# A fused two-block kernel: the low parts of the mixers' weights and three modulation vectors are made on GpSimd

## Time and profile before

| | |
|---|---|
| median of 3 runs | 1066.14 us (1065.88 to 1066.76) |
| the profiled execution | 1066.5 us, of which the span from first to last instruction is 1064.5 us |
| PE busy | 1027.7 us, 97% of the span |
| DVE busy | 700.2 us, 66% |
| ACT busy | 537.3 us, 50% |
| POOL busy | 39.0 us, 4% |
| DMA | 212.27 MB, mean 199 GB/s |

### The profile page before, as it was taken

One profiled execution on the slowest core, in us unless ns is written; L12 is line 12 of the kernel. 1 busy time (PEld: TensorE's weight loads), 2 busy tenths in 40 slices (PEclk: granted clock), 3 DMA queues, 4 the chain that ended last, 5 costly groups with the idle time before them and its releaser, 6 DMA issues.

```text
span 1064.5 us, 19831 instructions
## 1 busy us (share of the span) xinstructions
PE 1027.7 (97%) x8502; PEld 994.4 (93%) x8502; DVE 700.2 (66%) x1213; ACT 537.3 (50%) x903; POOL 39.0 (4%) x75
## 2 busy tenths in 40 slices
PE   5999999999988999999999999999999999999995
PEld 4899999988987899999999999999999999999985
DVE  3478886557687577776656778655457775555485
ACT  4453543455554655544444577554355554444453
POOL 5000000010000001000000000003000000000000
PEclk7999999999999999999999999999999999999998
DMA  9979889876734445577655456336156575565511
GB/s 304 380 251 318 310 319 322 287 247 204 212 109 159 157 144 155 197 244 271 205 191 183 135 178 218 120 123 175 60 163 216 187 237 164 194 198 163 195 40 40
DMA packets 144463, 212.27 MB, mean 199 GB/s; under 512 B 4259, under 2 KB 121239, under 8 KB 144376
## 3 DMA queue, kind: packets, MB, share of 16 engines
q1 hardware_dynamic: 138928, 194.40, 54.9%
q0 software_dynamic: 5184, 16.30, 4.8%
q10 hardware_dynamic: 264, 0.31, 0.1%
HBM read 209.88 MB, written 1.11 MB: 198 GB/s over the span
## 4 chain that ended last, share of the span: by engine, by line
PE 67%; issue 22%; DVE 7%; ACT 2%; DMA 1%; SPq 0%; POOL 0%; POOLq 0%; DVEq 0%; ACTq 0%
PE PS L460 65%; DVE wlo L1769 4%; PE PS L468 2%; DMA SC<-in_w_ada_dram 1%; ACT whi L1286 1%; DVE SC L1727 1%; DVE xT L1736 0%; DVE W L1727 0%; DVE hl L1736 0%; ACT SC L1278 0%; DVE st L1739 0%; DVE SC L1733 0%; DVE SS L1727 0%; ACT SC L1273 0%; DVE SC L2202 0%
## 5 line engine op out<-in xcount | busy, mean ns | idle before, releaser
L1769 DVE TENSOR_TENSOR wlo<-raw,whi 128x1024 fp32r<-128x1024 f32 (+2 forms) x331 | 386.8, 1186 | 203.2 <-ACT whi L1286 202.6
L1286 ACT ACTIVATE whi<-raw 128x1024 fp32r<-128x1024 f32 (+2 forms) x331 | 331.9, 1022 | 176.7 <-PE PS L460 137.7
L460 PE MATMUL PS<-hh,whi 128*128 128x256 f32 (+1 forms) x1376 | 393.8, 286 | 6.8 <-DVE wlo L1769 4.6
L460 PE MATMUL PS<-hh,wlo 128*128 128x256 f32 (+1 forms) x1376 | 388.6, 282 | 0.0
L460 PE MATMUL PS<-hl,whi 128*128 128x256 f32 (+1 forms) x1376 | 387.9, 282 | 0.0
L460 PE MATMUL PS<-SR,whi 128*128 128x256 f32 (+1 forms) x1824 | 329.1, 283 | 4.0 <-DVE wlo L1769 1.4
L460 PEld LDWEIGHTS PS<-SR,whi 128*128 128x128 f32 x1824 | 279.8, 188 | 8.9 <-issue 2.6
L460 PEld LDWEIGHTS PS<-hh,whi 128*128 128x128 f32 x1376 | 260.2, 189 | 12.8 <-DVE wlo L1769 6.5
L460 PEld LDWEIGHTS PS<-hl,whi 128*128 128x128 f32 x1376 | 261.0, 190 | 0.4
L460 PEld LDWEIGHTS PS<-hh,wlo 128*128 128x128 f32 x1376 | 260.8, 190 | 0.0
L460 PE MATMUL PS<-SR,wlo 128*128 128x256 f32 (+1 forms) x912 | 256.7, 281 | 0.0
(11 more groups left out here) (183 smaller groups left out, 714.5 us busy)
## 6 DMA issues: line engine op xcount, KB each, us to landing
raw<-in_ffn_w_dram SPq DMA_DIRECT2D x60, 1024.0 KB, 7.2
raw<-in_w_in_dram SPq DMA_DIRECT2D x38, 1024.0 KB, 5.4
raw<-in_w_ff_dram SPq DMA_DIRECT2D x32, 1024.0 KB, 5.3
raw<-in_w_ada_dram SPq DMA_DIRECT2D x16, 1024.0 KB, 6.6
SC<-in_w_ada_dram POOLq DMA_DIRECT2D x12, 1024.0 KB, 6.4
SC<-in_w_ada_dram SPq DMA_DIRECT2D x8, 1024.0 KB, 12.2
raw<-in_w_out_dram SPq DMA_DIRECT2D x8, 1024.0 KB, 4.9
raw<-in_ffn_w_dram SPq DMA_DIRECT2D x8, 768.0 KB, 12.6
```

Source lines behind the costliest of these rows:

```text
L460: return e.matmul(o, l, r, start=start, stop=stop, skip_group_check=True)
L1286: e.activation(hi_part(p), raw_part(p), ACT.Copy).then_inc(*hi_done.up(p.i))
L1769: e.tensor_tensor(lo_part(p), raw_part(p), hi32(hi_part(p)), ALU.subtract).then_inc(*lo_done.up(p.i))
```

## The change

- 113 of the 331 low parts are made by POOL, with the same subtraction: those of the first mixer from its third gate load on (43) and all of the second mixer (70). 103 of them are 128 x 1024, two are 128 x 768 and eight 128 x 256. They have a signal of their own, `lo_pool`. TensorE and SP wait for the one or the other by `low_signal`.
- Vectors 5, 6 and 7 are made on POOL as DVE makes 2, 3 and 4: for each row tile a multiplication by a column of `cact` in place, and an addition into `ada_buf[v]`, two instructions, of which the first tile of a vector needs only the multiplication. `pair_rows` is gone; TensorE does a `sum_rows` for each of the three.
- The loads of the pairs 2 to 11 are issued after the rows 0, 2, 4, ... of the first feed-forward (the last after row 18), and after POOL has used the slot.
- POOL's queue now holds, in order: constants and small loads; the twelve pairs, each with the load of the pair two later; a small memset; the low parts of the first mixer; the bias loads, with the low parts of the second mixer between them; the rest of the low parts; the last loads.

```
@@ -210,6 +209,7 @@
         for k in (0, 4):
             self.piece(c0, k, k + 4, 0, 256)
             self.piece(c1, k, k + 4, 0, 160)
+        self.on_pool = True
         for i in (2, 3, 4):
             self.tall("gate", w_in, GATE0 + 256 * i)
...
         self.row("out1", a["w_out"][0], 6)
+        self.on_pool = False
         for b in range(NB):
             self.block(1, w13[1], b)
...
+        self.on_pool = True
         for i in range(4):
             self.wide("qa", w_in2, QA + 256 * i)
...
         self.row("out2", a["w_out_2"][0], 6)
+        self.on_pool = False
         for j in range(18):
...
+        def low_signal(i):
+            return lo_pool if pieces[i].on_pool else lo_done
...
-                on.wait_ge(lo_done, p.i)
+                on.wait_ge(low_signal(p.i), p.i)
...
             def sum_rows(v, b, c):
-                on.wait_ge(dve_done, ("ada", v, 7))
+                on.wait_ge(pool_done if 5 <= v < 8 else dve_done, ("ada", v, 7))
...
-                if b > 6:
-                    pair_rows(5, b - 7, 7)
+                if b == 6:
+                    sum_rows(5, 7, 0)
...
-            on.wait_ge(dve_done, ("av", 0, 19))
-            pair_rows(6, 0, 5)
...
-            rows_end(todo, 0, lambda n: pair_rows(6, (n + 1) // 2, 5) if n in (1, 4, 6) else None)
+
+            def shift2_rows(n):
+                if n == 6:
+                    on.wait_ge(dve_done, ("av", 0, 19))
+                    sum_rows(6, 5, 0)
+
+            rows_end(todo, 0, shift2_rows)
...
-            on.wait_ge(dve_done, ("mean", 0))
-            for q in (0, 1):
-                pair_rows(7, q, 0)
...
-            for q in (2, 3):
-                pair_rows(7, q, 0)
+            on.wait_ge(dve_done, ("mean", 0))
+            sum_rows(7, 0, 0)
...
-            for n, u in enumerate(plan.rings["pair"]):
-                on.wait_ge(mm_done, plan.first_rows[5 + 2 * n].end if n < 2 else plan.rings["pair"][n - 2].end)
-                e.dma_start(ring_view(u), u.src).then_inc(*pair_in[u.slot].landed(u))
...
+            def lo_to(n):
+                while low["n"] < n:
+                    p = pieces[low["n"]]
+                    if p.on_pool:
+                        on.wait_ge(hi_done, p.i)
+                        e.tensor_tensor(lo_part(p), raw_part(p), hi32(hi_part(p)), ALU.subtract).then_inc(*lo_pool.up(p.i))
+                    low["n"] += 1
+
+            pairs = plan.rings["pair"]
+
+            def load_pair(n):
+                if n < 2:
+                    on.wait_ge(mm_done, plan.first_rows[5 + 2 * n].end)
+                else:
+                    on.wait_ge(mm_done, ("row", 0, 2 * n - 4 if n < 11 else NT - 4))
+                    on.wait_ge(pool_done, ("ada", 5 + (n - 2) // 4, 2 * ((n - 2) % 4) + 1))
+                e.dma_start(ring_view(pairs[n]), pairs[n].src).then_inc(*pair_in[pairs[n].slot].landed(pairs[n]))
+
+            load_pair(0)
+            load_pair(1)
+            on.wait_ge(act_done, "cact")
+            for n, u in enumerate(pairs):
+                v = 5 + n // 4
+                on.wait_ge(pair_in[u.slot], u)
+                for k in range(2):
+                    row = 2 * (n % 4) + k
+                    src, col, buf = ring_view(u)[:, k, :], cact[:, row:row + 1], ada_buf[v]
+                    if row:
+                        e.tensor_scalar(src, src, col, None, ALU.mult).then_inc(*pool_done.up(("times", v, row)))
+                        on.wait_ge(pool_done, ("times", v, row))
+                        e.tensor_tensor(buf, buf, src, ALU.add).then_inc(*pool_done.up(("ada", v, row)))
+                    else:
...
+                        e.tensor_scalar(buf, src, col, None, ALU.mult).then_inc(*pool_done.up(("ada", v, row)))
+                if n + 2 < len(pairs):
+                    load_pair(n + 2)
             on.wait_ge(dve_done, "rope", "axial")
             on.wait_ge(mm_done, ("ada_cols", 3))
             e.memset(cu[:, :, 0:2], 0.0).then_inc(*pool_done.up("pad"))
+            lo_to(split_at["acc", 1, 0][0])
...
                 if u >= 2:
+                    lo_to(split_at["s_b", u - 2][1])
                     on.wait_ge(dve_done, ("s_b", u - 2))
...
+            lo_to(len(pieces))
             on.wait_ge(dve_done, ("gm", 3, 7))
```

More of the change, by code:

```diff
@@ L113, with __init__ @@
 class Piece:
-    def __init__(self, i, load, k0, k1, c0, c1):
-        self.i, self.load, self.at, self.k, self.c = i, load, (k0, k1, c0, c1), k1 - k0, c1 - c0
+    def __init__(self, i, load, k0, k1, c0, c1, on_pool):
+        self.i, self.load, self.at, self.k, self.c, self.on_pool = i, load, (k0, k1, c0, c1), k1 - k0, c1 - c0, on_pool
 class Plan:
@@ L127, in __init__ @@
         self.rings = {"raw": [], "row": [], "pair": []}
-        self.first_rows, self.pairs = [], {}
+        self.first_rows, self.pairs, self.on_pool = [], {}, False
         self.lay_out(a)
@@ L137, in piece @@
     def piece(self, u, k0, k1, c0, c1):
-        self.pieces.append(Piece(len(self.pieces), u, k0, k1, c0, c1))
+        self.pieces.append(Piece(len(self.pieces), u, k0, k1, c0, c1, self.on_pool))
         u.end = ("lo", len(self.pieces) - 1)
@@ L562, in sum_rows @@
                 m.then_inc(*count(("ada_sum", v)))
[L564 to L571, removed]
             def sum_columns(vs, b):
@@ L1192, in sp_program @@
                     if old.end[0] == "lo":
-                        on.wait_ge(lo_done, old.end[1])
+                        on.wait_ge(low_signal(old.end[1]), old.end[1])
                     elif old.end[0] == "ada":
@@ L1386, in act_program @@
             hi_before(("ada_sum", 3))
-            ada_rows_out(5, 7, 0, ("pair", 5, 3), ("ada_sum", 4))
+            ada_rows_out(5, 7, 0, ("ada_sum", 4))
             ada_rows_out(4, 7, 256, ("ada_sum", 4))
@@ L1397, in act_program @@
                     on.wait_ge(dve_done, ("a", 0, NT - 1))
-                    ada_rows_out(6, 5, 0, ("pair", 6, 3))
+                    ada_rows_out(6, 5, 0, ("ada_sum", 6))
             hi_before(("g1", 0))
@@ L1410, in act_program @@
             hi_before("c_rows")
-            ada_rows_out(7, 0, 0, ("pair", 7, 3))
+            ada_rows_out(7, 0, 0, ("ada_sum", 7))
             on.wait_ge(mm_done, "c_rows", ("ada_col", 6))
@@ L1767, in lo_to @@
                         ada_sum()
-                    on.wait_ge(hi_done, p.i)
-                    e.tensor_tensor(lo_part(p), raw_part(p), hi32(hi_part(p)), ALU.subtract).then_inc(*lo_done.up(p.i))
+                    if not p.on_pool:
+                        on.wait_ge(hi_done, p.i)
+                        e.tensor_tensor(lo_part(p), raw_part(p), hi32(hi_part(p)), ALU.subtract).then_inc(*lo_done.up(p.i))
                     low["n"] += 1
@@ L2096, in dve_program @@
             last_one()
-            on.wait_ge(mm_done, ("pair", 7, 3))
             for t in range(2):
```

13 lines of the change are left out of this document (9 added, 4 removed).

## The result

The changed kernel takes 1116.75 us in the median of four runs (1114.66 to 1116.92), the kernel before 1066.2 us beside it: a ratio of 1.0469, 95% interval 1.0451 to 1.0487. The forecast was 1078 us and its range ended at 1092. It is slower by 50.6 us where 12 were forecast.

A forecast was written before the change was run, and what follows sets the result against it. The prediction took TensorE's work plus some 10 us of waits as the bound. It summed 1066.5 - 9.8 (pairs) + 16.6 (first feed-forward) + 0 + 5 (second mixer) = 1078.3, less 0.4 for the median: 1078 us, range 1048 to 1092.

The forecast's parts named there:

- Part 1: Twelve pairs leave TensorE and three row sums are added: net gain 9.8 us, 3.3 of it in the first feed-forward.
- Part 4, that the engines exclude each other: A POOL instruction reading SBUF and a two-SBUF-input DVE instruction exclude each other; the second is blocked until the first ends.
- Rival 1: Whole kernel: the engines don't hinder each other, so 1050 us, bounds 1047 and 1056; chance 0.34.
- rival 3: Second mixer: POOL is too slow for TensorE, over 2.86 us a low part; 1083 us at 3.3 us each; chance 0.07.
- Part 4, the first feed-forward: DVE's two-input work and POOL's 61.6 us exceed the 162.7 us stretch: 16.6 us lost, between 10.9 and 22.4.
- Part 5: Pair loads moved forward into the first feed-forward: cost 0, bound 4 us.
- Part 4, the second mixer: DVE's other work plus POOL's, 225.5 us for 218: 5 us lost, at least 0 and at most 7.5.
- Part 4, the first mixer: No lack of throughput, but small DVE steps can wait up to 2.2 us: 0, bounds of 5 either way.
- Part 2: POOL's prices: 1.1 us for one input, 2.2 us for two, so 6.6 us a pair and 61.6 us for ten.
- Rival 2: Whole kernel: partial hindrance, only some forms collide or they share by halves; about 1064 us, 1058 to 1068; chance 0.10.
- Rival 4: Relief of DVE is worth nothing outside the first mixer; alone, with the pairs' gain, 1056 us; chance counted in Rival 1.

The follow-up runs named there:

- Experiment 9: Experiment 1's kernel with each of POOL's multiplications and additions replaced by a memset of the same buffer: 1058.29 us, ratio 0.9916 to the kernel before.
- experiment 1: The changed kernel with all low parts back on VectorE, only the pairs (vectors 5, 6, 7) on POOL: 1082.0 us, ratio 1.0146 to the kernel before.
- experiment 8: The changed kernel with POOL's low parts cut into two halves (the eight of 128 x 256 stay whole): 1107.45 us, ratio 1.0397 to the kernel before.
- experiment 2: The kernel before with only the 113 low parts moved to POOL, the pairs still on TensorE: 1096.9 us, ratio 1.0285.

## Why the prediction was wrong, point by point

- **Part 1, the pairs leave TensorE, -9.8 us: right.** Experiment 9 has -9.0 us, 7.3 to 10.6. At its second milestone it is 7.1 us ahead: up to there TensorE waits 3.6 us in it, 1.4 before, so some 2 us of the gain come back as small waits.
- **Part 4, that the engines exclude each other: right in mechanism**, but for POOL's multiplication. Instructions of VectorE with two SBUF inputs grew beside POOL's reads, those with a PSUM input did not, and memsets did nothing. The Trainium skill ("SBUF — State Buffer", "Who interferes with whom") says the same of two-SBUF-input instructions, and that the fast mode of a one-input `tensor_scalar` contends as well; the 2851 ns beside 749 agree with it. The rule as the prediction gives it, that the one that comes second is blocked until the first has ended, holds here for POOL's subtractions and additions; beside its multiplications by a column VectorE was held up for about 1.0 of 2.85 us. Rival 1 (no hindrance, 1050 us) is false: VectorE's instructions did stretch. So is rival 3: 2.44 us a low part is below the 2.86 us of a piece, and nobody waited for POOL's low parts.
- **Part 4, the first feed-forward, +16.6 us: the number was right, 18.0 by experiments 1 and 9, but with luck.** It is a stretch bound by throughput: VectorE is busy 172.4 of 181 us. The sum took POOL's 61.6 us as its whole working time. But from 54 to 235 us of experiment 1 POOL ran 21 multiplications and 17 additions, 100 us even at their shortest (2.84 and 2.38 us), and the same sum with 100 us has 112 + 100 - 162.7 = 49 us at its low end. It came out near because two errors cancel: a multiplication takes 2.85 us and not 1.1, and hinders for only about 1.0 of them. Counted by what hinders, 21 x 1.0 + 17 x 2.4 is 62 us (an estimate from the rows of experiments 1 and 9), by chance the 61.6 on record.
- **Part 5, loads, 0: right**, as far as 0.6 us is no difference. ScalarE waits longer for raw loads in experiment 9 too, 45.6 us against 34.2 in the earlier trace rows, and nothing ends later for it.
- **Part 4, the second mixer, +5 us with a high bound of 7.5: this step failed.** It measured 18.9 us. The step took the sum of VectorE's other work and POOL's work, found it hardly over the 218 us, and priced the excess. But the mixer isn't bound by VectorE's throughput. It has short chains, on which TensorE waits for the last link, and a link waits for *one whole instruction of POOL*, however short it is itself, as long as POOL works without a gap. Eleven steps of a norm's reciprocal root, eight on 128 x 1 and three on 128 x 4 (the row names the first's shape), before:

```profile
616.48 1.85 DVE L1736 SCALAR_TENSOR_TENSOR sm<-sm 128x1 f32<-128x1 f32 x11
```

and after, with POOL's row beside it:

```profile
644.88 8.33 DVE L1778 SCALAR_TENSOR_TENSOR sm<-sm 128x1 f32<-128x1 f32 x11
```

```profile
642.42 9.40 POOL L1252 TENSOR_TENSOR wlo<-raw,whi 128x1024 fp32r<-128x1024 f32 x4 [8.97 <-ACT whi L1328]
```

1.85 us have become 8.33, and the difference is nearly three POOL instructions. TensorE waits 4.0 us behind it, until 653.99 us, 2.2 us after POOL's four. The longest wait of the mixer, 7.6 us, ends at 692.89 us, and the six low parts that POOL made in a row at 692.28.

- **Part 4, the first mixer, 0 us with bounds of 5: the same step, failed.** Its text had the right sentence ("each small step of DVE can wait up to 2.2 us") and didn't multiply it by the steps. It measured 11.5 us. Eight steps of the attention's norm, before:

```profile
295.57 0.48 DVE L1730 TENSOR_SCALAR st<-st 128x32 f32<-128x32 f32 x3
...
297.31 0.45 DVE L1736 SCALAR_TENSOR_TENSOR st<-st 128x48 f32<-128x48 f32 x2
```

after, beside the run of nine low parts shown under experiment 8:

```profile
321.15 5.07 DVE L1772 TENSOR_SCALAR st<-st 128x32 f32<-128x32 f32 x3
326.26 2.35 DVE L1769 TENSOR_TENSOR st<-st 128x48 f32<-128x48 f32 x1
328.64 4.59 DVE L1778 SCALAR_TENSOR_TENSOR st<-st 128x48 f32<-128x48 f32 x2
333.27 2.51 DVE L1769 TENSOR_TENSOR st<-st 128x48 f32<-128x48 f32 x2
335.81 0.45 DVE L1778 SCALAR_TENSOR_TENSOR st<-st 128x48 f32<-128x48 f32 x2
```

From the first to the start of the last row, eight steps took 1.7 us (295.57 to 297.31) and take 14.7 (321.15 to 335.81). Six waits of one POOL instruction, 2.35 us each (21.16 / 9), are 14.1. In experiment 8 the same eight steps take 9.6 us (319.26 to 328.82), but the steps behind them are held up there too. TensorE's wait of 9.3 us ends at 338.82 us, 3.4 us after POOL's nine. Counted so, from rows of before alone and the 2.2 us that the prediction assumed, these eight steps would have been priced at up to 8 x 2.2 = 17.6 us, and the chain at no more than POOL's run of work beside it. The move of the low parts off VectorE, the 58.2 us of the earlier trace rows, bought nothing against it.

- **A cost that no part had: the clock.** Between 54 and 1025 us the waits of before were at most 1.7 us, and the granted clock was 1.00 in each stage. Windows of five us around the wait in the first mixer:

```profile
330.00:335.00 5.00, 0.00 (x0) 0.00 (x0) 4.93 (x3) 0.63 (x1) 5.00 (x3) 0.79 0.80 220
335.00:340.00 5.00, 1.18 (x6) 1.12 (x7) 4.72 (x13) 0.00 (x0) 0.46 (x1) 0.50 0.57 191
340.00:345.00 5.00, 5.00 (x32) 4.86 (x31) 3.69 (x8) 1.37 (x2) 0.00 (x0) 0.69 0.00 0
345.00:350.00 5.00, 5.00 (x46) 5.00 (x45) 2.20 (x4) 3.44 (x6) 2.39 (x1) 1.00 0.02 3
```

In the 9.3 us in which TensorE waits, PEclk falls to 0.79 and then to 0.50 (1.2 of 2.4 GHz), and from 340 to 345 us, when TensorE is busy again, it is 0.69, with 32 matmuls started where the next five us have 46. That is 14 x 0.119 = 1.7 us for this one wait, an estimate, and an upper one: the five us after that have 41. Two such places in the second mixer show 0.79 with 36 and 0.69 with 33 matmuls where 45 follow, 1.1 and 1.4 us.

- **Part 2, POOL's price of a pair, 6.6 us: wrong.** The addition was near (2.2 forecast, 2.4 at its shortest). The multiplication by a column was taken by the memset's slope, 1.1 us with a bound of 2.3, and takes 2.84 at its shortest. The last four tiles, two pairs, show it:

```profile
233.03 3.49 POOL L1275 TENSOR_SCALAR SC<-SC,sm 128x1024 f32<-128x1024 f32 x1
...
253.04 2.37 POOL L1277 TENSOR_TENSOR SC<-SC 128x1024 f32<-128x1024 f32 x1
```

From 233.03 to 255.41 us POOL works without a gap, 11.2 us a pair. "Done near 220" became 255. So POOL's reads went on beside VectorE's serial end of the first feed-forward, where TensorE takes 42.8 us between the first two milestones in experiment 1 and 37.7 in experiment 9: 5.1 us lost.

**The sum once more**, at the milestones: -7.1 us (experiment 9 at the second one, 254.5 against 261.6), +23.1 for the pairs' collisions (experiment 1 against 9 at the same place: 18.0 + 5.1), +3.2 more there in the change than in experiment 1 (280.8 against 277.6), +11.5, +18.9 = +49.6. Some 1.2 of the 3.2 us stand in experiment 2 too, which has the low parts alone (43.3 us between the first two milestones, 42.1 before); the rest isn't assigned.

Against the sum on record (-9.8 + 16.6 + 5 = 11.8) that is 37.8 us more: 13.9 in the second mixer, 11.5 in the first, 8.3 between the first two milestones, and 4.1 from the smaller misses (2.7 that experiment 9 is short of the 9.8 at the second milestone, and 1.4 in the first feed-forward). Rival 2 had the right sentence ("only some forms collide") with the wrong price. Rival 4 is true as far as it goes: the relief of VectorE was worth nothing; but it wasn't alone.

**What stays open.** Of the 11.5 us in the first mixer, PE's idle time explains 8: it is idle 17.2 of 189 us from 281 to 470 us, against 9.2 of 178 from 262 to 440 in the execution before. In the other 3.5 PE is busy for longer; the clock explains at most 1.7 of them by the row above, the rest isn't assigned to rows. Experiment 8 won 4.2 us in the second mixer and 0.8 in the first; the runs of POOL explain why the long waits stayed, not where in the second mixer the 4.2 us come from. That TensorE's long waits end with POOL's runs is read from the traces; no run changed how far ahead POOL may work, and none put memsets in place of the mixers' low parts, as experiment 9 does for the pairs. Whether POOL's multiplication is slow by itself or because it fetches the column was not tried.

## What to carry to other kernels

Before work is moved to GpSimd, list what VectorE does meanwhile in short serial steps with its inputs in SBUF, and price each step at one whole GpSimd instruction, up to the length of GpSimd's uninterrupted run of work beside the chain; a sum of busy times prices only stretches that are bound by throughput, and only if it takes the time for which an instruction hinders, not the time for which it runs. The relief of an engine that isn't waited for buys nothing, and its neighbour's instructions can take more from it than was taken off: here 113 instructions fewer and 51 us more. Where VectorE has slack, give it the work (0.3% faster here); where GpSimd must work beside it, let it do so beside steps that read PSUM. Cutting its instructions in half won back 7 to 9 us of 50 here; the traces suggest that keeping it idle during the chain would win more, which no run tried.

## What the runs showed of the hardware that was not expected

- GpSimd's multiplication of 128 x 1024 float32 by a column of scalars, one tensor input, takes 2.86 us, longer than an addition or subtraction of two tensors (2.4 us), a copy (1.49 us in the mean, hindered ones included) or a memset (0.955 us). One input isn't always cheaper than two.
- Beside that multiplication, VectorE's instructions with two inputs in SBUF were held up for about the first 1.0 us of its 2.85; beside an addition or subtraction, for all of it.
- A VectorE step of 128 x 1 can wait as long as one of 128 x 1024: up to 2.4 us in all for 0.21 us of work.
- A one-input multiplication on VectorE, 749 ns alone, took 2851 ns beside POOL's subtractions (one instruction) and 1766 ns in the mean of three beside its multiplications and additions.
- After waits of 4 to 9 us TensorE came back at less than its full clock (0.69 and 0.79 granted in the first five us), and that cost 1.1 to 1.7 us each time, on top of the wait.
